# The last block's entry joined and begun on unnormalised input, the normalised one put in behind it

## What is computed

```python
mod = jax.nn.silu(c) @ w_mod[l] + b_mod[l]
sh_m, sc_m, gt_m, sh_f, sc_f, gt_f = ...
h = rms_norm_2(x, g_mix_norm[l]) * (1.0 + sc_m) + sh_m
proj = h @ w_in[l]
(q_a, k_a, v_a, q_i, k_i, w_i, q_b, k_b, v_b, gate_a, gate_b) = jnp.split(proj, split_at, axis=-1)
...
logits = jnp.einsum('bqhd,bsd->bqhs', qib, ki)
score = jnp.einsum('bqh,bqhs->bqs', wib, jax.nn.relu(logits))
score = jnp.where((key_pos[None, :] <= t[:, None])[None], score, NEG)
_, sel = lax.top_k(score, topk)            # 64 of 256
```

## Time and profile before

| | us |
|---|---|
| median of three executions | 1475.35 |
| lowest, highest | 1466.58, 1475.72 |
| span of the profiled execution, first to last instruction | 1468.2 |
| TensorE busy | 1446.1 (98%) |
| weight loads of TensorE busy | 1406.6 (96%) |
| VectorE busy | 1056.6 (72%) |
| ScalarE busy | 700.0 (48%) |
| GpSimd busy | 29.0 (2%) |

### The profile page before, as it was taken

How to read it: one execution, slowest core, us unless ns; L and a number is a source line. 1 busy time by engine, 2 the same in 40 slices (tenths; PEclk the granted TensorE clock), 3 DMA queues, 4 the chain that set the end, 5 groups by cost and what they waited for, 6 DMA issues and landing times. The chain is left out here.

```text
span 1468.2 us, 28465 instructions
## 1 busy us (share of the span) xinstructions
PE 1446.1 (98%) x11585; PEld 1406.6 (96%) x11585; DVE 1056.6 (72%) x1439; ACT 700.0 (48%) x910; POOL 29.0 (2%) x58
## 2 busy tenths in 40 slices
PE   8999999999999999999999999999999999999999
PEld 8999999999999999999999889999987899999999
DVE  6766779777667786677878768767887777876652
ACT  6544353454443454443554655443436766544431
POOL 0000100000001000001000000001000000000000
PEclk9999999999999999999999999999999999999999
DMA  9555835437447644458343226647633436365540
GB/s 324 220 187 186 268 149 201 172 106 267 172 172 249 239 173 172 171 196 288 128 173 124 78 70 246 227 173 268 234 115 135 145 139 231 131 228 185 184 173 30
DMA packets 42538, 269.09 MB, mean 183 GB/s; under 512 B 4768, under 2 KB 5920, under 8 KB 13520
## 3 DMA queue, kind: packets, MB, share of 16 engines
q1 hardware_dynamic: 33984, 240.31, 45.1%
q0 software_dynamic: 7312, 26.44, 5.5%
q10 hardware_dynamic: 1152, 1.05, 0.2%
HBM read 266.73 MB, written 1.05 MB: 182 GB/s over the span
## 5 line engine op out<-in xcount | busy, mean ns | idle before, releaser
L418 PE MATMUL ps<-x_hi,w_hi 128*128 128x272 f32 (+2 forms) x2296 | 661.8, 288 | 6.7 <-DVE x_lo L1447 1.9
L420 PE MATMUL ps<-x_hi,w_lo 128*128 128x272 f32 (+2 forms) x2296 | 651.8, 284 | 0.0
L419 PE MATMUL ps<-x_lo,w_hi 128*128 128x272 f32 (+2 forms) x2296 | 651.7, 284 | 0.0
L2024 ACT ACTIVATE w_hi<-raw_weights 128x2048 fp32r<-128x2048 f32 x219 | 416.9, 1912 | 291.6 <-PE ps L420 289.0
L1174 DVE TENSOR_TENSOR w_lo<-raw_weights,w_hi 128x2048 fp32r<-128x2048 f32 x193 | 439.7, 2288 | 143.8 <-ACT w_hi L2024 143.3
L418 PEld LDWEIGHTS ps<-x_hi,w_hi 128*128 128x128 f32 x2296 | 433.1, 189 | 10.8 <-DVE x_lo L1380 2.5
L419 PEld LDWEIGHTS ps<-x_lo,w_hi 128*128 128x128 f32 x2296 | 433.3, 189 | 0.7
L420 PEld LDWEIGHTS ps<-x_hi,w_lo 128*128 128x128 f32 x2296 | 433.1, 189 | 0.0
L418 PE MATMUL ps<-a_hi,w_hi 128*128 128x272 f32 x592 | 169.6, 286 | 0.0
L419 PE MATMUL ps<-a_lo,w_hi 128*128 128x272 f32 x592 | 169.6, 286 | 0.0
L420 PE MATMUL ps<-a_hi,w_lo 128*128 128x272 f32 x592 | 169.6, 286 | 0.0
(11 more groups left out here) (259 smaller groups left out, 1543.9 us busy)
## 6 DMA issues: line engine op xcount, KB each, us to landing
raw_weights<-w_units SPq DMA_DIRECT2D x226, 1024.0 KB, 4.9
mod_w<-mod_units POOLq DMA_DIRECT2D x48, 512.0 KB, 5.5
raw_weights<-w_units SPq DMA_DIRECT2D x4, 256.0 KB, 5.8
raw_weights<-w_units SPq DMA_DIRECT2D x2, 512.0 KB, 9.2
out<-h ACTq DMA_DIRECT2D x8, 128.0 KB, 1.9
h<-x_in SPq DMA_DIRECT2D x2, 272.0 KB, 4.1
h<-x_in SPq DMA_DIRECT2D x1, 544.0 KB, 8.0
tab<-tables POOLq DMA_DIRECT2D x1, 512.0 KB, 7.9
```

What stands on the lines that cost most here:

```text
L418: pe.matmul(dst, wh, hi, start=start, stop=False)
L419: pe.matmul(dst, wh, lo, start=False, stop=False)
L420: return pe.matmul(dst, wl, hi, start=False, stop=stop)
L2024: act.activation(w_hi[:, u % RING, :], raw[:, u % RING, :], ACT.Copy).then_inc(S["hi_ready"], 1)
```

## The change

One group of six tiles takes the place of `small_group` and `group` 0. Its input is h times the gain, unnormalised, with two shift columns. The factor and the shift's share are put in when its tiles are evicted. The second statistics, both long fillers and the full normalisation inside the seam go. The rows groups still want normalised input: during rows 0 `full`, `whole`, `whole_hi` and `full_lo` make it, over the place of the unnormalised one. The jobs of rows 0 move to rows 1, others behind them by one to three tiles; the attention scores of groups 8 and 9 move two tiles later. Table scaling moves from VectorE to ScalarE.

```diff
@@ counts: w_in now uses 16 x tiles; side bank 3, spread bank 2 @@
@@ TensorE @@
-            stats(stages["down", 3], w_in, filler=60)
-            stats(stages["down", 3], w_in, evict=False, filler=10)
-            def small_group(): ...
+            stats(stages["down", 3], w_in)
+            def entry_groups():
+                pe.wait_ge(S["lo_ready"], u + 2)
+                pe.wait_ge(S["x_hi_ready"], X0["w_in"] + 1)
+                for m in range(2):
+                    hi_passes(*small(0, m), x_hi[:, 0, 0:C])          # C = SEQ + 2
+                for m in range(GROUP):
+                    hi_passes(*query(0, m), x_hi[:, 0, 0:C])
+                for k in range(KT):
+                    if k == 4:
+                        pe.wait_ge(S["lo_ready"], u + 3)
+                    pe.wait_ge(S["x_ready"], X0["w_in"] + k + 1)
+                    ...                    # small tiles, then query tiles, three passes each
+                    if 1 <= k < 5:
+                        mod_sums(3, side_bank(w_in), range(3 * k - 3, 3 * k))
+                    if k == 5:
+                        row_sums(SEQ, side_bank(w_in))
@@ rows() @@
-                    if half == 1:
+                    if half == 1 and j > 0:
+                        if j == 0 and qt == 0:
+                            pe.wait_ge(S["x_ready"], X0["w_in"] + KT + k + 1)
-            small_group()
-            group(w_in, 0, xs, between={1: [lambda: key_and_weights()]})
-            rows(0, {0: rotate_qi(0), 1: rotate_qi(1), 2: turn_tab(0),
-                     3: idx_scores(0), 4: turn_tab(1), 6: idx_scores(1)})
-            rows(1, {0: turn_tab(2), 1: turn_tab(3), 2: idx_scores(2)})
-            rows(2, {2: turn_rows(0, 0), 4: turn_rows(0, 1)})
+            entry_groups()
+            rows(0, {7: key_and_weights()})
+            rows(1, {0: turn_tab(0), 1: rotate_qi(0), 2: rotate_qi(1), 3: turn_tab(1),
+                     4: idx_scores(0), 5: turn_tab(2), 6: idx_scores(1), 7: turn_tab(3)})
+            rows(2, {1: idx_scores(2), 4: turn_rows(0, 0), 6: turn_rows(0, 1)})
             paired(w_in, 8, ...
-                3: scores2(4), 5: scores2(5), turn_p2(4), 6: values2(4), 7: scores2(6), turn_p2(5)
+                5: scores2(4), 7: scores2(5), turn_p2(4)
             paired(w_in, 9, ...
-                0: values2(5), 1: scores2(7), turn_p2(6), 2: values2(6), 4: turn_p2(7), 5: values2(7)
+                0: values2(4), 1: scores2(6), turn_p2(5), 2: values2(5),
+                3: scores2(7), turn_p2(6), 4: values2(6), 6: turn_p2(7), 7: values2(7)
@@ VectorE: tail() with pieces of low parts at m = 2, 4, 7, 8, 9; then @@
             split_to(u0 + 4)
-            mod_evict(3, 2); copies to ki, wi_T; split_to(u0 + 5); rotation(ki)
-            scale_tables(); split_to(u0 + 6); store(0, qi)
+            entry_root()                        # reciprocal of the root, 128 x 256
+            entry_evict(pair_a, t0, 0, 4)       # small tiles times the factor
+            full(0); full(1); full(2); full_lo(0); full(3); full_lo(1); low_half()
+            full(4); full_lo(2); low_half(); full(5); full_lo(3); full(6); full_lo(4)
+            full(7); full_lo(5); full_lo(6); full_lo(7)
+            mod_evict(3, side_bank(w_in))
+            with_shift(ki[:, :], pair_a, 0)
+            with_shift(wi_T[:, :], pair_a, 1).then_inc(S["entry_ready"], 1)
+            entry_evict(pair_b, t0 + 4, 4, 2); entry_evict(pair_a, t0 + 6, 6, 2)
+            split_to(u0 + 6); rotation(ki); four with_shift() to qi; low_half()
             rotation(work1, 1, qi, 0); low_half(); rotation(work1, 1, qi, 1); low_half(); idx_add(0)
             low_half(); low_half(); idx_add(1); low_half()
-            low_half()
             idx_add(2)
-            take_best(0, TOPK // 8 - 3)
+            low_half()
             row_rope(0, 0); low_half(); row_rope(0, 1)
-            low_half()
             row_roots(0); low_half()
-            take_best(0, 3)
+            take_best(0, TOPK // 8)
             low_half()
@@ ScalarE: tail() with pieces of high parts at m = 2 to 5; then @@
+            scale_tables()
+            wide_root(SEQ, side_bank(w_in))
+            split_to(w_in.u0 + 5)
+            act.wait_ge(S["tile_done"], w_in.t0 + 2 * GROUP)
+            for m in range(KT + 1):
+                if m < KT:
+                    whole(m)                    # f = f * gain + shift
+                if m >= 1:
+                    whole_hi(m - 1)             # x_hi = f
             split_to(w_in.u0 + 6)
-            split(); store_tab(0); relu(0); store_tab(1); split(); relu(1)
-            store_v2(0); store_v2(1); store_tab(2); store_tab(3); split(); relu(2); split()
-            row_squares(0, 0); row_squares(0, 1); row_std(0)
+            split(); store_v2(0); store_v2(1); store_tab(0); split(); store_tab(1); relu(0)
+            store_tab(2); relu(1); split(); store_tab(3); split()
+            row_squares(0, 0); row_squares(0, 1); relu(2); row_std(0)
+            split()
             split(); store_rows(0, 0); split(); store_rows(0, 1)
```

More of the change, by code:

```diff
@@ L961, in small_group @@
-                    if 1 <= k < 7:
-                        mod_sums(3, 2, range(2 * k - 2, 2 * k))
+                    if k == 0:
+                        for dst, slot, col in [small(0, m) for m in range(2)] + [query(0, m) for m in range(GROUP)]:
+                            pe.matmul(dst, w_hi[:, slot, col:col + P], x_lo[:, 0, 0:C], start=False, stop=False)
+                    else:
+                        for m in range(2):
+                            ins = three_pass(*small(k, m), x_hi[:, k, 0:C], x_lo[:, k, 0:C], False, k == KT - 1)
+                            if k == KT - 1:
+                                ins.then_inc(S["tile_done"], 2)
+                        for m in range(GROUP):
+                            ins = three_pass(*query(k, m), x_hi[:, k, 0:C], x_lo[:, k, 0:C], False, k == KT - 1)
+                            if k == KT - 1:
+                                ins.then_inc(S["tile_done"], 1)
+                        if k == 3:
+                            ins.then_inc(S["weights_used"], 1)
@@ L1388, in update_and_prepare @@
                     return
[L1389 to L1408, removed]
+                squares_done()
             def before_evictions(nx, part=None):
@@ new lines, in entry_evict, with with_shift, full @@
+            def entry_evict(pair, t, bank, k):
+                dve.wait_ge(S["tile_done"], t + k)
+                dve.tensor_tensor(pair[:, :, 0:SEQ + 2], ps[:, bank:bank + 2, 0:SEQ + 2], bcast(rstd, SEQ + 2),
+                                  ALU.mult).then_inc(S["tile_evicted"], k)
+            def with_shift(dst, pair, j):
+                return dve.tensor_scalar(dst, pair[:, j, 0:SEQ], pair[:, j, SEQ:SEQ + 1], None, ALU.add)
+            def full(m):
+                dve.tensor_tensor(f[:, m, 0:SEQ], h[:, m, META:TOK], rstd[:, 0:SEQ], ALU.mult).then_inc(S["full_ready"], 1)
@@ new lines, in full_lo @@
+            def full_lo(m):
+                dve.wait_ge(S["x_hi_ready"], c.up("x_hi_ready"))
+                dve.tensor_tensor(x_lo[:, m, 0:SEQ], f[:, m, 0:SEQ], x_hi[:, m, 0:SEQ].bitcast(F32),
+                                  ALU.subtract).then_inc(S["x_ready"], 1)
+            u0, t0 = w_in.u0, w_in.t0
+            split_to(u0 + 4)
+            entry_root()
+            entry_evict(pair_a, t0, 0, 4)
+            full(0)
+            full(1)
+            full(2)
+            full_lo(0)
+            full(3)
@@ new lines, in _ @@
+            full_lo(1)
+            low_half()
+            full(4)
+            full_lo(2)
+            low_half()
+            full(5)
+            full_lo(3)
+            full(6)
+            full_lo(4)
+            full(7)
+            full_lo(5)
+            full_lo(6)
+            full_lo(7)
+            mod_evict(3, side_bank(w_in))
+            dve.wait_ge(S["tile_evicted"], w_in.evicted(t0 + 4))
+            with_shift(ki[:, :], pair_a, 0)
+            with_shift(wi_T[:, :], pair_a, 1).then_inc(S["entry_ready"], 1)
@@ L2124, in prepare @@
                         high_piece()
[L2125 to L2130, removed]
+                c.up("sq_used", 6)
             def before_evictions(nx, bank):
@@ L2446, in _ @@
             row_squares(0, 1)
+            relu(2)
             row_std(0)
+            split()
             split()
```

148 lines of the change are left out of this document (82 added, 66 removed).

## The result

The changed kernel took 1498.39 us (median of four executions, 1492.68 to 1502.17) against 1474.1 us of the kernel before: a ratio of 1.0178, 95% interval 1.0154 to 1.0203. That is 24.3 us between the medians and 26.2 us by the ratio. The forecast of 1489.6 had the sign, but its size was 9 us short, and the result lies 1.4 us above the range of 1476 to 1497. The profiled executions differ by 1490.5 - 1468.2 = 22.3 us. That of the changed kernel is the fastest of its four; what the other three took beyond it, 4 to 10 us, is in no trace.

The account below looks back on a forecast made before the run. TensorE's own work was taken to bound the kernel from 1090 us on. Seam -8.9, VectorE +8.9 and +1.3, ScalarE +11.3, clock +1.7: +14.3 on the profiled 1468.2, plus 7.15 to the median: 1489.6 us, range 1476 to 1497.

Parts of the forecast that it names:

- The entry: Last block's seam up to the rows: first product at 1060.6, rows from 1083.4 instead of 1092.3, 8.9 us gained.
- the new wait: Ahead of rows 0, TensorE stands 2.5 us for the normalised input.
- VectorE takes the gain back: At the row turns TensorE waits 3.6 us (first) and 5.7 (third) for VectorE; the 8.9 are spent, 1.3 more lost.
- ScalarE's lead: Behind row_std(0) ScalarE runs one unit further ahead, so its later items wait for slots; 11.3 us in sum.
- group 9: TensorE waits there for a low part behind its peak on VectorE: 2.1 us, 2.65 with the half unit ahead of group 8.
- the second branch: It waits for its bank because unit 27 and the first eviction slip: 1.45 us.
- The clock: One fall to half speed, behind the longest new pause, costing 1.7 us.
- The third: Rival: the clock falls at most pauses, three more falls on the critical queue, +5 us, 1494; chance 0.18.
- The first rival: The gain is kept at the row turns and copies of p: -7 us, 1468; chance 0.10.
- The second: Rival: VectorE takes the gain back, ScalarE's lead is hidden: +1.3 and 2.65 of group 9, 1479; chance 0.17.
- the fourth: Rival: the entry doesn't start earlier, the seam stays and all terms but the first add, 1497; chance 0.02.

Follow-up runs that it names:

- e3: Changed kernel with products of no use filling five of TensorE's pauses, each lot shorter than its pause; 1487.65 us, ratio 1.0119.
- e4: Changed kernel with VectorE's best-of search moved out from between the two ropes of rows and spread behind them; 1498.81 us, ratio 1.0178.
- e1: Changed kernel with one of the two split() behind row_std(0) taken out, so ScalarE runs no unit ahead; 1486.6 us, ratio 1.0105.
- e6: e5 with the best-of search spread as in e4 and relu(2) ahead of the split and the row squares; 1473.23 us, ratio 1.0036.
- e10: e9 with ScalarE's split of unit 8 ahead of relu(0), later splits one place earlier, one VectorE half unit ahead of idx_add(0); 1464.65 us, ratio 0.9963.
- e2: Kernel before with only a second split() behind row_std(0), so ScalarE runs one unit ahead; 1491.49 us, ratio 1.0154.
- e5: e1 with the attention jobs of groups 8 and 9 at the places of the kernel before; 1474.18 us, ratio 1.0039.
- e9: e6 with 17 products of no use ahead of rows 0, row turns behind tile 6 of rows 2 and 0, 3, 6 of rows 3; 1467.8 us, ratio 0.9979.

## Why the prediction was right in kind and short in size

**The entry** held in each step: the first product 4.0 us behind the statistics (4.5 forecast), rows at 27.1 behind them (27.3), the new wait 2.4 (2.5). One number in it doesn't add up: 12 products of 0.117 before 1080.9 are 1079.5, not 1079.8; the rows would have come out 0.3 earlier by it, at the 27.0 that the trace nearly has.

**VectorE takes the gain back** held too: 3.5 us at the first turn (3.6), 3.8 at the third (5.7). With the fall that eats 1.7 of the latter's cover it is 5.5, as e3 shows. It landed 1.5 late, 1.3 was forecast. But e4 shows that the wait there has two sources: with the search out of the way, the bank copy behind ScalarE's extra unit holds the turn almost as long. The forecast had only the first, so its landing was right partly by luck.

**ScalarE's lead** held place by place: 1.2, 2.4, 2.4 and 1.0 measured against 1.35, 2.5, 2.5 and 0.85, and e1 takes out these and the late bank. The forecast priced it at 11.3 with group 9 and the second branch; the waits behind the third turn grew by 13.9. The 2.6 over are group 9, 3.5 where the forecast had 2.1 of its 2.65, and two more waits for evictions of gate groups, 0.9 and 0.6 (the rest of the row of 5.1), which it hadn't at all. Of group 9 the step reads "the low part of a unit whose second half stands behind its peak", and it forgot the eviction that stands behind that half. The late bank of the second branch was 1.2 (1.45).

**The clock** is the step that failed. "I take one, behind the longest pause: 1.7." There were four falls, and 6.4 us of them counted, 4.7 more than forecast; e3 gives 3.9 (by the traces) to 8.7 (by the times) back by keeping TensorE at work in the same pauses. By the sum: 14.3 + 0.2 + 2.6 + 4.7 and the 1.5 that only an estimate places = 23.3. I had priced the clock from the two falls of an execution in which TensorE never waits longer than 1.9 us. That was evidence on its own pauses, not on longer ones.

**The rivals.** The third, a fall at most pauses, was to be held right at three falls behind 1080; there were four. Its +5 was the right size (4.7). The forecast's waits and this rival's clock are both true, and should have been one case. The Trainium skill (TensorE: Matmul & The Clock Gate, HAM oscillation) says that idle stretches between groups of products send the engine back to half clock each time. The trace agrees in the main: from the entry on falls came at pauses of 3.5, 3.8, 2.4 and 3.5, none at those of 1.2 and 1.0 and at the other two of 2.4. The first rival's point, the gain kept, is reached only in part once both queues are repaired: seam to FFN is 1.2 us shorter than before in e6 and 4.1 in e10, of the 9.1 won at the entry. The second (the lead is hidden) falls with e1 and e2; the fourth with the first product at its forecast place.

## What to carry to other kernels

When a list of a side engine gets one more item that is never taken out again, every later item waits for a resource that comes free one step later: count it along the whole list, since here this alone cost 22.7 us with the falls of the clock that it brought. Price a chain of new pauses together with the clock that they lower. A pause can be filled with products into a bank that is free anyway, if they end before the release. To keep a gain made at a seam, look first at which queues stood just behind the engine before it.

## What the runs showed of the chip that was not expected

The pauses of 3.5 us brought falls of either length. Ahead of group 9 it was 6.8 us at half clock in the changed kernel and e1, and 3.4 in e4; at the first row turn 6.8 in e4 and e5, and 3.4 in the changed kernel and e1. What decides between them isn't shown.

A stage without waits and at full granted clock can take two times. The 528 products of the last stage took 62.07 us in the profiled executions of the kernel before, e1 and e5 and 59.7 in the other ten. The 192 of `w_out`, ahead of the FFN, took 22.7 in those of the kernel before, e1, e3, e5 and e9 and 21.9 in the other eight. In both stages the products of one execution stand evenly, 0.118 us apart or 0.113. So 2.3 us of a difference between two profiles can come from a stage that no edit touches, which is why the sums here end at the FFN, and up to 0.8 is left in them even so.
